# Modulation summed in PSUM, four first units, tanh in the unit's own bank: a hybrid attention and DeltaNet block

## The reference, cut to what matters

```python
mod = c @ w_ada + b_ada
shift, scale, gate = jnp.split(mod, 3, axis=-1)
h = rmsnorm(x, pre_norm_gain) * (1.0 + scale[:, None, :]) + shift[:, None, :]
proj = h @ w_in                    # 15 parts: aq ak av az iq ik iw bq bk bv bz bbeta ba ga gb
# branch A: rope, an indexer that picks 128 keys a query, softmax attention, times silu(az), @ w_a_out
o_a = dsa_attention(qa, ka, va, q_idx, k_idx, iw)
y_a = (o_a * silu(az)) @ w_a_out
# branch B: depthwise convolution of width 4 and silu on bq, bk, bv, then the chunked gated delta rule
qkv = silu(causal_depthwise_conv(concat([bq, bk, bv]), dn_conv_w))
o_b = gated_delta_rule_chunked(l2norm(cq) * d ** -0.5, l2norm(ck), cv, g, beta)
y_b = (rmsnorm(o_b, dn_norm_gain) * silu(bz)) @ w_b_out
out = (sigmoid(ga) * y_a + sigmoid(gb) * y_b) @ w_o
return x + gate * rmsnorm(out, post_norm_gain)
```

## Time and profile before

| | us |
|---|---|
| median of 3 runs | 833.03 (831.88 to 834.09) |
| the profiled execution, own time | 835.1 |
| its span, first to last instruction | 833.3 |
| TensorE busy | 787.4 (94%) |
| VectorE busy | 451.6 (54%) |
| GpSimd busy | 406.6 (49%) |
| ScalarE busy | 338.1 (41%) |
| mean granted TensorE clock | 0.984 of full |

### The profile page before, as it was taken

The page is one execution under the profiler, slowest core; times in us unless marked ns, Lnnn a source line. Parts: engine busy times, 40 slices in busy tenths (PEclk is TensorE's granted clock), DMA queues, the critical chain, the costliest instruction groups (busy, mean ns, idle before and its releaser), DMA issues.

```text
span 833.3 us, 11212 instructions
## 1 busy us (share of the span) xinstructions
PE 787.4 (94%) x4048; PEld 639.5 (77%) x4048; DVE 451.6 (54%) x976; ACT 338.1 (41%) x719; POOL 406.6 (49%) x346
## 2 busy tenths in 40 slices
PE   2889897999998999999999999999999999999997
PEld 1667774688887788888888777787787788878997
DVE  5985896955786776668573343433343332322113
ACT  5445644634435254443542544434333323112231
POOL 3565543464535355456454452654455345534551
PEclk9899998999999899999999999999999999999999
DMA  9823647443334233221312212221321244542502
GB/s 332 340 98 139 222 105 180 133 121 121 96 94 86 76 96 101 89 90 60 105 52 84 70 50 76 77 74 53 101 76 51 77 176 161 181 138 76 207 23 101
DMA packets 69350, 95.58 MB, mean 115 GB/s; under 512 B 32920, under 2 KB 45592, under 8 KB 69296
## 3 DMA queue, kind: packets, MB, share of 16 engines
q1 hardware_dynamic: 69296, 94.88, 35.2%
HBM read 85.08 MB, written 9.22 MB: 113 GB/s over the span
## 4 chain that ended last, share of the span: by engine, by line
PE 70%; DVE 19%; ACT 4%; DMA 3%; issue 2%; SPq 0%; POOL 0%; DVEq 0%; POOLq 0%; ACTq 0%
PE ps L729 16%; PE ps L731 16%; PE ps L730 16%; DVE mod_rows L1606 5%; PE ps L998 2%; PE ps L1052 2%; PE ps L1051 2%; PE ps L1050 2%; PE ps L985 2%; ACT prob L1318 2%; DVE kraw L1757 1%; DVE prob L1940 1%; DVE binv L1815 1%; DVE score L1728 1%; DVE binv L1833 1%
## 5 line engine op out<-in xcount | busy, mean ns | idle before, releaser
L1416 POOL TENSOR_TENSOR w_lo<-raw,w_hi 128x512 fp32r<-128x512 f32 x208 | 283.2, 1385 | 299.1 <-ACT w_hi L1070 299.0
L729 PE MATMUL ps<-h_hi,w_hi 128*128 128x512 f32 x640 | 272.3, 425 | 1.1 <-DVE kraw L1757 1.1
L731 PE MATMUL ps<-h_hi,w_lo 128*128 128x512 f32 x640 | 252.0, 394 | 0.0
L730 PE MATMUL ps<-h_lo,w_hi 128*128 128x512 f32 x640 | 251.4, 393 | 0.0
L729 PEld LDWEIGHTS ps<-h_hi,w_hi 128*128 128x128 f32 x640 | 121.4, 190 | 31.7 <-issue 10.0
L731 PEld LDWEIGHTS ps<-h_hi,w_lo 128*128 128x128 f32 x640 | 121.0, 189 | 27.4
L730 PEld LDWEIGHTS ps<-h_lo,w_hi 128*128 128x128 f32 x640 | 121.7, 190 | 21.6 <-issue 2.2
L1070 ACT ACTIVATE w_hi<-raw 128x1024 fp32r<-128x1024 f32 x104 | 108.6, 1054 | 17.1 <-PE ps L1052 17.1
L1254 ACT ACTIVATE o_tok<-ps 128x128 f32<-128x128 f32 x32 | 8.9, 277 | 97.4 <-PE ps L950 97.3
L1606 DVE SCALAR_TENSOR_TENSOR mod_rows<-mod_rows,pcol 128x256 f32<-128x256 f32 x56 | 42.8, 772 | 2.3 <-ACT mod_rows L1087 0.4
L1051 PE MATMUL ps<-w_lo,y_hi 128*128 128x256 f32 x128 | 36.2, 283 | 0.0
(11 more groups left out here) (275 smaller groups left out, 1409.5 us busy)
## 6 DMA issues: line engine op xcount, KB each, us to landing
raw<-in_w_units SPq DMA_DIRECT2D x104, 512.0 KB, 3.3
mod_rows<-in_w_mod SPq DMA_DIRECT2D x16, 512.0 KB, 8.1
inverse_tiles<-zero SPq DMA_DIRECT2D x12, 344.0 KB, 5.2
ada<-in_w_gate SPq DMA_DIRECT2D x8, 512.0 KB, 4.6
first_raw<-in_w_first SPq DMA_DIRECT2D x8, 320.0 KB, 5.7
x_sb<-in_x SPq DMA_DIRECT2D x4, 512.0 KB, 5.5
L<-gc_rows SPq DMA_DIRECT2D x8, 256.0 KB, 4.6
lower_tiles<-L SPq DMA_DIRECT2D x8, 256.0 KB, 2.8
```

Source lines behind the costliest of these rows:

```text
L729: pe.matmul(out_ap, w_hi[:, slot, k, :], rhs_hi(k), start=(k == 0), stop=False)
L730: pe.matmul(out_ap, w_hi[:, slot, k, :], rhs_lo(k), start=False, stop=False)
L731: mm = pe.matmul(out_ap, w_lo[:, slot, k, :], rhs_hi(k), start=False, stop=(k == KT - 1))
L1416: ins = pool.tensor_tensor(w_lo[:, slot, ks], raw[:, slot, ks], w_hi[:, slot, ks].bitcast(F32), ALU.subtract)
```

## The change

- `N_FIRST` is 4: S, K0, K1, K2 are first units and K3 is a full unit, multiplied in rounds 0 to 3 into bank 4; I0 goes into bank 5. Every later unit keeps its place among the units, and so has a round number greater by 4.
- `mod_sum` keeps its running sum in PSUM (banks 4 and 5, by turns); ScalarE's first product goes there, and only the last link writes `mod_rows` for TensorE. The columns of `modulation` go to the same banks behind the sum; ScalarE's first product of step k waits for the scale column of step k - 2.
- The tanh of keys, queries and values goes to the unit's own PSUM bank, where `swish` reads it. A unit's bank counts as left when the swish is done, no longer at the third tap. The waits that guarded `tz` between heads are gone. The counters of keys are split into `key_tap`, `key_act`, `key_dve` and `key_sw`.
- Round numbers change: key taps (`R_TAP`, new), `R_KEY`, `R_LOW`, `R_GRAM`, `R_INV`, `R_PAIR`, `R_TURN`, `R_LOGIT`, `R_DECAY`; the index key's norm moves from rounds 1 and 2 to 9 and 11 (`R_LN`), and `SELECTS` moves selections from heads 1 and 2 to heads 3 and 5.
- In the prologue ScalarE's sine stands before all four squares, no longer between the second and the third.

```diff
-N_FIRST = 5
+N_FIRST = 4
...
-R_KEY = [1, 4, 7, 10] + [ends_at("K", h) for h in range(4, HEADS)]
-R_LOW = [8, 9, 10, 11, 22, 25, 38, 42]
-R_GRAM = [9, 10, 12, 16, R_DELTA[0] + 1, R_DELTA[0] + 6, R_DELTA[1] + 3, R_DELTA[1] + 7]
-R_INV = [20, R_DELTA[1] + 12]
+R_TAP = [0, 0, 0, 5] + [ends_at("K", h) for h in range(4, HEADS)]
+R_KEY = [1, 2, 4, 8] + [ends_at("K", h) for h in range(4, HEADS)]
+R_LOW = [6, 9, 10, 11, 22, 25, 38, 42]
+R_GRAM = [9, 10, 12, 16, R_DELTA[0] + 1, R_DELTA[0] + 7, R_DELTA[1] + 3, R_DELTA[1] + 7]
+R_INV = [23, R_DELTA[1] + 13]
...
-R_PAIR = [[R_STORE[0] + n for n in (8, 9, 10, 12, 13, 14, 16, 17)], [R_DELTA[2] + n for n in (12, 14, 16, 18, 20, 24, 26, 27)]]
+R_PAIR = [[R_STORE[0] + n for n in (8, 9, 10, 12, 13, 14, 16, 17)], [R_DELTA[2] + n for n in (14, 15, 17, 19, 21, 24, 26, 27)]]
-R_TURN = ends_at("I", 3) + 4
-R_LOGIT = [R_DELTA[0] - 16 + 14 * (m // 2) // 11 for m in range(24)]
-R_DECAY, R_IKEY = 6, 18
+R_TURN = ends_at("I", 3) + 7
+R_LOGIT = [R_DELTA[0] - 14 + 14 * (m // 2) // 11 for m in range(24)]
+R_SOFT, R_DECAY, R_LN, R_IKEY = 3, 5, 9, 18
-SELECTS = [0, 1, 2, 2, 2, 3, 3, 3]
+SELECTS = [0, 0, 1, 3, 2, 4, 3, 3]
...
-        return {"S": (small_act, "smT"), "K": (key_dve, "3"), "I": (iq_act, "q"), "GA": (ga_act, "t"), "Q": (q_dve, "3"),
-                "V": (v_dve, "3"), "Z": (z_dve, "s"), "AQ": (aq_act, "c"), "AK": (ak_act, "c"), "AV": (av_act, "c"),
+        return {"S": (small_act, "smT"), "K": (key_sw, "s"), "I": (iq_act, "q"), "GA": (ga_act, "t"), "Q": (q_dve, "s"),
+                "V": (v_dve, "s"), "Z": (z_dve, "s"), "AQ": (aq_act, "c"), "AK": (ak_act, "c"), "AV": (av_act, "c"),
...
-            pe.wait_ge(*key_dve.at("s", h))
+            pe.wait_ge(*key_sw.at("s", h))
+            if h == 0:
+                take_wait(pe, 5)
...
+        act.wait_ge(*pro_dve.at("clampc"))
+        act.activation(rsc[:], rred[:], ACT.Sin).then_inc(*pro_act.inc("sin"))
         for i in range(NT):
-            if i == 2:
-                act.wait_ge(*pro_dve.at("clampc"))
-                act.activation(rsc[:], rred[:], ACT.Sin).then_inc(*pro_act.inc("sin"))
...
-            act.activation(mod_rows[:, k % GROUPS, 0, :], mod_rows[:, k % GROUPS, 0, :], ACT.Copy,
+            if k >= 2:
+                act.wait_ge(*pro_dve.at(f"scale{k - 2}"))
+            act.activation(ps[:, 4 + k % 2, 0:2 * P], mod_rows[:, k % GROUPS, 0, :], ACT.Copy,
                            scale=pcol[:, 0, R_C:R_C + 1]).then_inc(*pro_act.inc(f"row{k}"))
...
-                act.activation(tz[:, 1, :], kraw[:, h, :], ACT.Tanh, scale=0.5).then_inc(*key_act.inc("tanh"))
+                act.activation(bank(unit_bank("K", h)), kraw[:, h, :], ACT.Tanh, scale=0.5).then_inc(*key_act.inc("tanh"))
...
-            acc = mod_rows[:, k % GROUPS, 0, :]
+            acc = ps[:, 4 + k % 2, 0:2 * P]
...
-                dve.scalar_tensor_tensor(out=acc, in0=mod_rows[:, k % GROUPS, j, :], scalar=pcol[:, 0, R_C + j:R_C + j + 1], in1=acc,
-                                         op0=ALU.mult, op1=ALU.add).then_inc(*pro_dve.inc(f"row{j}_{k}"))
+                total = mod_rows[:, k % GROUPS, 0, :] if j == KT - 1 else acc
+                dve.scalar_tensor_tensor(out=total, in0=mod_rows[:, k % GROUPS, j, :], scalar=pcol[:, 0, R_C + j:R_C + j + 1],
+                                         in1=acc, op0=ALU.mult, op1=ALU.add).then_inc(*pro_dve.inc(f"row{j}_{k}"))
...
-                swish(key_dve, key_act, kraw[:, h, :], tz[:, 1, :], h)
+                swish(key_sw, key_act, kraw[:, h, :], bank(unit_bank("K", h)), h)
```

More of the change, by code:

```diff
@@ L417, in program @@
     ga_act = steps("ga_act", ["t"])
-    key_act = steps("key_act", ["tap", "tanh"])
-    key_dve = steps("key_dve", ["1", "2", "3", "s"])
+    key_tap = steps("key_tap", ["tap"])
+    key_act = steps("key_act", ["tanh"])
+    key_dve = steps("key_dve", ["1", "2", "3"])
+    key_sw = steps("key_sw", ["s"])
     low_act = steps("low_act", ["y", "d"])
@@ L744, in part @@
             kind = UNITS[q][0]
-            if quarter == 0:
+            if quarter == 0 and q >= 2 * PROJ_BANKS:
                 take_wait(pe, before_in_bank(q))
@@ L781, in modulation @@
                 pe.wait_ge(*pro_pool.at("ones"))
[L782 to L783 removed]
             pe.wait_ge(*pro_dve.at(f"row{KT - 1}_{k}"))
             for n in range(2):
[L786 removed]
+                mm = pe.matmul(ps[:, 4 + k % 2, 2 * P + n:2 * P + n + 1], mod_rows[:, k % GROUPS, 0, n * P:(n + 1) * P], ones_p[:, 0:1],
                                start=True, stop=True)
@@ L1204, in rows @@
                 act.wait_ge(*q_dve.at("3", h))
-                if h >= 1:
-                    act.wait_ge(*v_dve.at("s", h - 1))
-                act.activation(tz[:, 0, :], yq[:], ACT.Tanh, scale=0.5).then_inc(*q_act.inc("tanh"))
+                act.activation(bank(unit_bank("Q", h)), yq[:], ACT.Tanh, scale=0.5).then_inc(*q_act.inc("tanh"))
             elif rel == 8:
@@ L1215, in rows @@
                 act.wait_ge(*v_dve.at("3", h))
-                act.wait_ge(*q_dve.at("s", h))
-                act.activation(tz[:, 0, :], yv[:], ACT.Tanh, scale=0.5).then_inc(*v_act.inc("tanh"))
+                act.activation(bank(unit_bank("V", h)), yv[:], ACT.Tanh, scale=0.5).then_inc(*v_act.inc("tanh"))
             elif rel == 12:
@@ L1375, in _ @@
                 rows(h, r - R_DELTA[h])
-                key(h, r - R_KEY[h])
+                key(h, r)
                 attention_rows(h, r)
@@ L1657, in small @@
                                          op0=ALU.mult, op1=ALU.max).then_inc(*small_dve.inc("az"))
[L1658 to L1662, removed]
+            elif r == 1:
                 dve.wait_ge(*small_act.at("tanh"))
@@ L1693, in small @@
                     *small_dve.inc("nbegc"))
+            elif r == R_LN:
+                dve.tensor_reduce(small_cols[:, 32:36], sm[:, :, 0:IDX_DIM], AX_X, ALU.add).then_inc(*small_dve.inc("mu"))
+                dve.wait_ge(*small_dve.at("mu"))
+                dve.tensor_scalar(small_cols[:, 32:36], small_cols[:, 32:36], 1.0 / IDX_DIM, None, ALU.mult).then_inc(
+                    *small_dve.inc("mus"))
+                dve.wait_ge(*small_dve.at("mus"))
+                dve.tensor_tensor(cent[:], sm[:, :, 0:IDX_DIM], per_tile(small_cols[:, 32:36], IDX_DIM),
+                                  ALU.subtract).then_inc(*small_dve.inc("cent"))
+                dve.wait_ge(*small_dve.at("cent"))
+                dve.tensor_tensor(csq[:], cent[:], cent[:], ALU.mult).then_inc(*small_dve.inc("csq"))
+                dve.wait_ge(*small_dve.at("csq"))
+                dve.tensor_reduce(small_cols[:, 36:40], csq[:], AX_X, ALU.add).then_inc(*small_dve.inc("var"))
+                dve.tensor_scalar(sm[:, :, SM_IW:SM_IW + IDX_HEADS], sm[:, :, SM_IW:SM_IW + IDX_HEADS], IDX_HEADS ** -0.5,
+                                  None, ALU.mult).then_inc(*small_dve.inc("iw"))
+            elif r == R_LN + 2:
+                dve.wait_ge(*small_pool.at("rstd"))
+                for n in range(2):
+                    dve.tensor_tensor(kdup[:, :, n * IDX_DIM:(n + 1) * IDX_DIM], cent[:],
+                                      per_tile(small_cols[:, 40:44], IDX_DIM), ALU.mult).then_inc(*small_dve.inc(f"kd{n}"))
             elif r == R_IKEY:
@@ L1777, in rows @@
             elif rel == 7:
-                swish(q_dve, q_act, yq[:], tz[:, 0, :], h)
+                swish(q_dve, q_act, yq[:], bank(unit_bank("Q", h)), h)
             elif rel in (8, 9):
@@ L1781, in rows @@
             elif rel == 11:
-                swish(v_dve, v_act, yv[:], tz[:, 0, :], h)
+                swish(v_dve, v_act, yv[:], bank(unit_bank("V", h)), h)
             elif rel == 13:
```

56 lines of the change are left out of this document (19 added, 37 removed).

## The result

The changed kernel takes **819.08 us** (median of 4 runs, 818.74 to 819.72) against 833.56 for the kernel before on the same chip: a ratio of **0.983, 95% interval 0.981 to 0.985**. That is 14.5 us or 1.7%: clear of the noise, and less than 2%. The forecast was 814, its range 804 to 825, its own case 809 to 819.

The account below looks back on a forecast made before the run. TensorE bounds the kernel, losing time to waits, half clock and a prologue paced by VectorE. Terms -13.4 + 5.5 - 4.6 - 6.9 + 0.3 = -19.1 took the median from 833.0 to 814 us, range 804 to 825.

Parts of the forecast that it names:

- its own case: Whole kernel: the forecast's main case, 809 to 819 us, given a chance of 0.54 against the rivals.
- Links in PSUM: Prologue: modulation-sum multiply-adds in PSUM at 0.57 us each, a step 4.2 us, rounds starting at 53.4 instead of 66.8: -13.4.
- The start: Prologue's beginning: the sine moved ahead puts tables about 2 us earlier; step 0's columns at 18.0 instead of 21.3 us.
- K3 and the rounds: Rounds to the first query unit: K3 as a full unit costs +5.5 us; changed waits and half clock give -4.6.
- the grams behind keys: Early rounds: TensorE's waits of 1.75 and 1.40 us for the swish of keys 2 and 3 were to vanish.
- the 4.36: Rounds before about 168 us: TensorE's 4.36 us wait of logits behind VectorE's scores, with its half clock, was to go.
- 200 to 290 us: Heads 1 to 3: later corners of the second inversion and fewer selections in heads 1 and 2 were to give -6.9 us.
- I leave 2.0 of 8.9: From 200 us to 285 us: of 6.0 us waits and 2.9 us half clock, only 2.0 us were to stay.
- The old 3.48: Head 2's scan: TensorE's 3.48 us wait, blamed on VectorE idling for pair_b at the first corner, with 2.9 us half clock.
- Tanh into the bank: Units of keys, queries and values: tanh in PSUM was to cost nothing, and contended multiplies of up to 1.70 us go.
- prologue bound by DMA or TensorE: Rival, prologue: late weights or half clock make a step 4.8 us, 4 us more, total 818; chance 0.15.
- One of my signs of being wrong: Changed profile: links of 0.7 us or more, half-clock stretches still three in number, or new waits past 300 us.

Follow-up runs that it names:

- the sum that goes back and forth: Changed kernel with the modulation sum's links alternately reading PSUM and writing SBUF, then the reverse: 820.46 us, ratio 0.983 to the kernel before.
- The late corner alone: Changed kernel with one corner product of the second inversion in round 23 of head 2 instead of 21: 815.75 us, ratio 0.980 to the kernel before.

## Why the prediction was right, and where it wasn't

- **Links in PSUM.** The mechanism is shown by the sum back in SBUF and by the sum that goes back and forth. I took a link at 0.57 us and a step at 4.2. A link cost 0.49, and the step is 3.67, because TensorE, which I had counted as the faster one at 3.7, sets the pace. The 65 ns more a link of the Trainium skill, "Perfetto Trace Analysis", section Optimizing Scalar/DVE Operations, are not borne out.
- **The start.** Step 0's columns were due at 18.0 and came at 18.3. The sine did not put it 2 us earlier, as the prediction has it: the first weights' transfer holds it. Steps 1 and 2 took 4.7 and 5.3 us while TensorE ran at half clock, 2.6 us over the pace where I had 0.9. The last columns came at 46.6 where I had 48.3, and 5.4 us followed them where I had 5.1. The prologue gave 14.6 for 13.4, a faster pace and a slower start taken together.
- **K3 and the rounds.** Up to head 0's key transposes waits and half clock cost 12.0 us before (8.6 + 3.4, the clock being 0.77 from 130 to 145 us) and 8.7 now (5.3 + 3.4): -3.3 where I had -4.6. The unit's bank, the grams behind keys and the 4.36 vanished as forecast, gram 0 waited 2.2 where I had 3.1, the logits of round 45 waited 2.0 where I had 3.2. What I had too low is half clock: two stretches stood where I gave one half a chance. Four logit matmuls, about 1.0 us, now fall behind the mark at head 0.
- **200 to 290 us: the step that failed.** "I leave 2.0 of 8.9." The old 3.48 and its half clock (3.4 us lost, where I had 2.9) did go; 0.45 stands there. The reason that I gave, the later corners, is not borne out by the run with their old rounds. And I looked no further along the queue. The moved corner, now in round 21, met a GpSimd split in the same round as the taps of head 3 and one of its added selections, straight ahead of the third vnew: a wait of 2.07 and 1.7 of half clock, 13 us behind the old one. With 0.98, 0.71 and 0.45 the stretch keeps 5.9 us, not 2.0. The late corner alone takes 4.1 us away between heads 3 and 4, which is shown. The selections, which I credited, were part of the queue ahead and no gain. From waits and clock the stretch should have gained 4.2 less the 1.0 of the logits; it gained 2.1. Over both stretches together 0.4 us is unexplained.
- **Tanh into the bank.** No cost, as forecast, and no gain either: twice measured.
- **Rivals.** None came true as described. The total fell 5 us above the forecast, near "prologue bound by DMA or TensorE" (818). TensorE does pace the steps, but at 3.67 us and not at 4.8, and the prologue was faster than forecast: a total near a rival's number is no evidence for the rival. One of my signs of being wrong did come true: three half-clock stretches follow waits of the rounds, 5.1 us in all, where there were two of 3.4.
- **Where the 5.2 us of the miss are.** 3.1 lie between the traces (816.0 forecast, 819.07 measured for the profiled execution): 4.8 lost from head 0 to head 4, 1.7 won elsewhere. The other 2.1 come from the last step of the sum. I worked 19.1 us out on an execution of 835.1 and took it off a median of 833.0; by their granted clocks, given above, its shorter executions hold less lost time, so there was less to gain from the median. That the total lies no further off is in part luck: the 1.2 us that the prologue gained beyond the forecast hide as much of the loss.

## What to carry to other kernels

Where VectorE and GpSimd work side by side and a VectorE operation with two tensor inputs in SBUF is on the chain of waits, put one of the inputs into PSUM; here it cost next to nothing and was worth two thirds of the gain. Off the chain, as with the tanh, the same move gained nothing. When you price the removal of a wait by moving work in a written order, list what the moved piece now stands ahead of, with its contended duration, up to the next instruction that TensorE waits for. And weigh waits by size: in this kernel most of those of 2 us cost 3.7, while two of 1.3 and 1.2 cost 2.5.

## What the hardware did that I had not expected

- Lost clock comes in portions. Behind the waits of 4.36 and 3.48 us in the kernel before, 3.4 us each are lost; behind waits of 1.90 to 2.44 us in the rounds, 1.7 us in 23 of 26 cases over ten traces, and nothing in the other three. Behind waits of 1.75 us and less nothing, in the rounds of every trace; but in the prologue with the sum in SBUF a stretch of 1.7 us (52 to 57 us) follows a row of waits of 0.7. Why the three were spared no run tells.
- The two profiles of the changed kernel agree to 0.2 us in nearly every wait, and the clock fell behind the same three. Their spans differ by 1.2 us: 0.4 before the rounds and 1.0 between heads 3 and 4 (less 0.2 elsewhere), where the wait of 0.45 is missing in the second and the 2.07 is 1.90. The cause shows in who was held up: in the first VectorE's ob_lo and the corner behind it took 1.64 and 1.77 us beside a pair of GpSimd's splits of 3.01; in the second they took 0.68 each and the pair 4.24. So which of the two engines is delayed changes from execution to execution.
- Multiply-adds of 128x256 that read and write one PSUM bank, six in a chain, take 0.49 us each, as in SBUF.
